# A fused block with 256 expert gathers: head 0's expert numbers written in two eights, two groups of queries moved between the sums, gather buffers in another order, tile 1's steps at other ticks, the last gather in half rows

## The chip, the cores and the metric

The kernel runs on one core of one Trainium2 chip. The metric is device time in microseconds (us) of one execution; lower is better. All arithmetic is float32.

## The reference

Two transformer blocks run one after the other on 256 tokens of width 1024. Only the end of the second block matters here, the feed-forward layer with product keys. Each token has 8 heads. For each head, the query is scored against two tables of 128 keys, the best 16 of each table are combined to 256 candidates, and the best 16 candidates name 16 of 16,384 experts. An expert is a row `u` and a row `v` of 1024 floats each.

```python
def peer_ffn(h, w_q, keys1, keys2, u, v):
    ...
        q = (hc @ w_q).reshape(-1, PEER_HEADS, PEER_KEY_DIM).astype(jnp.float32)
        s1 = jnp.einsum('chd,nd->chn', q[..., :half], k1)
        s2 = jnp.einsum('chd,nd->chn', q[..., half:], k2)
        v1, i1 = lax.top_k(s1, PEER_TOPK)
        v2, i2 = lax.top_k(s2, PEER_TOPK)
        cand_s = (v1[..., :, None] + v2[..., None, :]).reshape(*v1.shape[:-1], PEER_TOPK * PEER_TOPK)
        cand_i = (i1[..., :, None] * N_KEYS + i2[..., None, :]).reshape(*i1.shape[:-1], PEER_TOPK * PEER_TOPK)
        best_s, best_pos = lax.top_k(cand_s, PEER_TOPK)
        expert = jnp.take_along_axis(cand_i, best_pos, axis=-1)
        g = jax.nn.softmax(best_s, axis=-1)
        act = jax.nn.gelu(jnp.einsum('cd,chkd->chk', hc, u[expert],
                                     preferred_element_type=jnp.float32), approximate=False)
        wgt = (g * act).astype(hc.dtype)
        return jnp.einsum('chk,chkd->cd', wgt, v[expert])
```

## The kernel before

The 256 tokens are two tiles of 128 rows, tile 0 and tile 1. The first half of the program computes the first block and the attention of the second block for tile 0. Then the expert stage of tile 0 starts, and the rest of tile 1 (its projections, its attention, its output projection, its queries) is threaded between the expert steps.

**A set.** The unit of the expert stage is a set `n` (0 to 255): one expert for each of 128 tokens. Sets 0 to 127 are tile 0's (head 0's 16 experts are sets 0 to 15, head 1's are 16 to 31, and so on), sets 128 to 255 are tile 1's. A set passes four engines: GpSimd (POOL) issues a gather (L2431) that fetches 128 rows of 8 KB, `u` and `v` side by side, 1 MB in all; VectorE (DVE) takes the dot product of the `u` half with the token (L2244); ScalarE (ACT) takes its gelu (L1439); GpSimd writes a diagonal matrix with gelu times softmax weight (L2403); TensorE (PE) multiplies the `v` half by that diagonal and adds it to a bank of psum (L1036, the set's "sum", four matmul records of 512 columns).

**Buffers.** A gather needs a free buffer, a slot. `slot_table` hands out the slots in order: `SLOTS` is 7 at first, and `JOIN` says before which set more are added (one before set 7, three before 88, two before 118). A slot comes free when its sum is done (`pe_used`). The first slots are a buffer of their own (`first_slot`), then halves of weight buffers that are free once their last user on TensorE is done: two in `wr0` after the output projection (`wout_ready`), two in `wr1` after the queries of heads 2 and 3 (`pq01`), two in `wr2` after the queries of heads 6 and 7 (`pq03`), then `xc`, free after `h2_done`. `pq02` and `pq03` are the queries of heads 4, 5 and 6, 7 of tile 0; both read `wr2`.

**GpSimd's queue.** GpSimd issues in program order, and a wait of one gather holds all that follow. Before it issues a gather into a slot whose last set was `before`, it has written the diagonals up to `before + LEAD`, that is `before + 2`:

```python
                while before is not None and laid <= before + LEAD:
                    expert_diagonal(laid)
                    laid += 1
```

**Ticks.** The order on TensorE, ScalarE and VectorE is written by hand. `until(tick)` on VectorE does the dot products of all sets below `tick`; on ScalarE the gelus of sets below `tick - 1`; on TensorE the sums of sets below `tick - 2`. Between calls of `until` stand the steps of tile 1. `att_tick(step)` places the ten steps of its attention, `T_TURN` the two transposes `mb1` and `ma1` of its result, `T_WOUT` its output projection and `T_QUERY` its queries.

**Expert numbers.** `route(head, step)` on VectorE is the selection for one head in 17 steps. Steps 0 to 6 find the best 8 candidates, steps 7 to 9 (L2158 to L2165) the next 8, steps 10 to 16 (L2168 to L2192) turn the 16 positions into expert numbers; step 16 signals `eid_done`. Head 0 runs through all steps before the first gather; head 1's steps 0 to 8 stand before the dot product of set 0 and the rest between those of sets 0 to 4. The weights of head 0's softmax (`softmax_sum`, L2200 to L2206, signal `norm_done`) stand before the dot product of set 2, and the first diagonal waits for them.

## Time and profile before

| | |
|---|---|
| median of 3 runs | 1464.35 us (1464.03 to 1465.04) |
| the profiled execution, its own time | 1460.45 us |
| its span in the profile | 1458.4 us |
| mean granted TensorE clock | 0.985 of full speed |
| HBM read over the span | 424.05 MB |
| TensorE busy | 1330.5 us (91%) |
| VectorE busy | 860.1 us (59%) |
| GpSimd busy | 430.8 us (30%) |
| ScalarE busy | 284.8 us (20%) |

Busy time is that of the whole span. All times in the rows below count from the start of the span. "DMA share" is the mean busy share of the core's 16 DMA engines, and GB/s is what they moved; a stretch at a share of 1.00 or 1.01 and about 425 GB/s is one in which they never ran dry. One gather of 1,048,576 bytes at 425 GB/s is 2.47 us.

### The profile page before, as it was taken

The numbers are of one execution on the slowest core, as the hardware profiler recorded it, in microseconds if no ns is written. First come the engines' busy times: TensorE is split into PE (matmuls) and PEld (weight loads), VectorE is DVE, ScalarE is ACT, GpSimd is POOL, SyncE is SP. The second block draws the span as 40 slices with busy tenths as digits, with TensorE's granted clock in tenths as the row PEclk, the third lists the DMA queues.
The fourth block names the chain that finished last, engine by engine and source line by source line (L and its number), as shares of the span: only waits on it lengthen the run. The fifth ranks groups of instructions, "written<-read, shape, count | busy, mean of one in ns | idle before, by whom it ended". The sixth has DMA issues, their size and how long they took to land.

```text
span 1458.4 us, 14811 instructions
## 1 busy us (share of the span) xinstructions
PE 1330.5 (91%) x5269; PEld 863.7 (59%) x5269; DVE 860.1 (59%) x2028; ACT 284.8 (20%) x680; POOL 430.8 (30%) x547
## 2 busy tenths in 40 slices
PE   7999999999999999999998999988998777777786
PEld 6887888898868777767566644445552222222222
DVE  3558461236117888844357668775666677766654
ACT  2123101032010000013423124531221112111101
POOL 0002000120001000000005445664556555655551
PEclk9999999999999999999899999998999999999999
DMA  8343533311366888767339999998999999999995
GB/s 284 118 173 116 218 130 115 116 59 58 128 231 241 290 291 297 267 216 289 116 124 420 423 424 422 422 417 353 425 425 426 425 426 425 426 425 426 426 425 250
DMA packets 119369, 426.10 MB, mean 292 GB/s; under 512 B 10674, under 2 KB 34680, under 8 KB 84224
## 3 DMA queue, kind: packets, MB, share of 16 engines
q0 software_dynamic: 37072, 270.59, 44.4%
q1 hardware_dynamic: 82224, 154.57, 29.5%
q8 instruction: 42, 0.69, 0.2%
q14 instruction: 31, 0.25, 0.0%
HBM read 424.05 MB, written 1.08 MB: 292 GB/s over the span
## 4 chain that ended last, share of the span: by engine, by line
PE 61%; DMA 29%; ACT 3%; DVE 3%; issue 2%; POOL 2%; SPq 0%; POOLq 0%; DVEq 0%; ACTq 0%
PE psum L563 30%; DMA wr<-peer_uv,arena 13%; DMA arena<-peer_uv,arena 8%; PE psum L1036 7%; DMA xc<-peer_uv,arena 4%; PE psum L811 4%; DMA first_slot<-peer_uv,arena 3%; PE psum L888 2%; PE psum L787 2%; PE psum L861 1%; PE psum L608 1%; PE psum L1186 1%; POOL arena L2403 1%; PE psum L1054 1%; PE psum L1007 1%
## 5 line engine op out<-in xcount | busy, mean ns | idle before, releaser
L563 PE MATMUL psum<-hT,wr 128*128 128x256 f32 x1792 | 389.8, 379 | 1.6 <-DVE hT L1592 1.6
L563 PEld LDWEIGHTS psum<-hT,wr 128*128 128x128 f32 x1792 | 339.8, 190 | 50.8 <-issue 5.3
L1036 PE MATMUL psum<-wr,arena 128*128 128x512 f32 x576 | 279.3, 615 | 39.5 <-POOL arena L2403 39.3
L2244 DVE CUSTOM_DVE_ANT_0 wr<-psum,wr 128x1024 f32<-128x1024 f32 x144 | 176.1, 1223 | 118.2 <-DMA wr<-peer_uv,arena 117.6
L1036 PEld LDWEIGHTS psum<-wr,arena 128*128 128x128 f32 x576 | 102.9, 193 | 180.8 <-issue 179.9
L2403 POOL TENSOR_SCALAR arena<-cst,arena 128x128 f32<-128x128 f32 x256 | 121.9, 476 | 193.5 <-ACT arena L1439 187.7
L2431 POOL DMA_INDIRECT wr<-peer_uv,arena x144 | 143.9, 999 | 75.0 <-PE psum L1036 47.4
L1036 PE MATMUL psum<-arena 128*128 128x512 f32 x256 | 125.8, 616 | 33.6 <-POOL arena L2403 33.6
L1439 ACT ACTIVATE arena<-arena 128x1 f32<-128x1 f32 x256 | 50.9, 202 | 504.3 <-DVE arena L2244 503.9
L2244 DVE CUSTOM_DVE_ANT_0 arena<-psum,arena 128x1024 f32<-128x1024 f32 x64 | 78.4, 1224 | 55.1 <-DMA arena<-peer_uv,arena 55.1
L1036 PEld LDWEIGHTS psum<-arena 128*128 128x128 f32 x256 | 44.0, 190 | 111.4 <-issue 111.2
L2386 POOL TENSOR_TENSOR arena<-arena 128x512 f32<-128x512 f32 x11 | 16.9, 1536 | 217.4 <-DVE arena L1607 217.4
L1887 DVE SCALAR_TENSOR_TENSOR arena<-arena,csil 128x512 f32<-128x512 f32 x96 | 79.2, 825 | 3.0
L1605 DVE TENSOR_SCALAR arena<-psum,vec 128x256 f32<-128x256 f32 x68 | 29.7, 479 | 86.4 <-PE psum L563 78.5
L1607 DVE SCALAR_TENSOR_TENSOR arena<-psum,vec,arena 128x255 f32<-128x255 f32 (+1 forms) x160 | 69.8, 477 | 2.8
L2431 POOL DMA_INDIRECT arena<-peer_uv,arena x64 | 64.2, 1003 | 15.7 <-issue 12.4
L2374 POOL TENSOR_TENSOR arena<-arena,xc 128x512 f32<-128x512 f32 x12 | 17.0, 1445 | 167.6 <-PE psum L710 133.7
L2431 POOL DMA_INDIRECT first_slot<-peer_uv,arena x24 | 24.0, 1000 | 129.7 <-DVE arena L2192 116.5
L811 PE MATMUL psum<-wr,arena 128*128 128x512 f32 x128 | 55.6, 592 | 0.0
L563 PE MATMUL psum<-arena,wr 128*128 128x256 f32 x256 | 55.4, 379 | 0.0
L1036 PE MATMUL psum<-first_slot,arena 128*128 128x512 f32 x96 | 47.7, 621 | 7.1 <-POOL arena L2403 7.1
L563 PEld LDWEIGHTS psum<-arena,wr 128*128 128x128 f32 x256 | 48.6, 190 | 7.0 <-issue 0.5
(332 smaller groups left out, 1548.4 us busy)
## 6 DMA issues: line engine op xcount, KB each, us to landing
wr<-in_w_in SPq DMA_DIRECT2D x22, 2048.0 KB, 8.3
arena<-in_w_ada SPq DMA_DIRECT2D x12, 2048.0 KB, 9.7
wr<-in_w_up SPq DMA_DIRECT2D x22, 1024.0 KB, 7.8
arena<-piece SPq DMA_DIRECT2D x16, 1024.0 KB, 9.0
wr<-in_w_down SPq DMA_DIRECT2D x5, 2048.0 KB, 9.5
wr<-in_w_a_out SPq DMA_DIRECT2D x2, 2048.0 KB, 8.0
wr<-in_w_b_out SPq DMA_DIRECT2D x2, 2048.0 KB, 8.4
wr<-in_w_o SPq DMA_DIRECT2D x2, 2048.0 KB, 7.7
```

Source lines behind the costliest of these rows:

```text
L563: mm = nc.tensor.matmul(bank[p % 4][:, f * S:(f + 1) * S], slot(i)[:, k, c:c + P], act[:, k, :], start=k == 0, stop=k == KT - 1)
L787: mm = nc.tensor.matmul(bank[4 + 2 * n + t][:, :], sgb[:, k, t * P:(t + 1) * P], slot(23 + n)[:, k, :], start=k == 0, stop=k == KT - 1)
L811: mm = nc.tensor.matmul(bank[4 + 2 * n + t][:, :], act_ffn[:, f, t * P:(t + 1) * P], slot(i)[:, row, n * BANK:(n + 1) * BANK], start=f == ...
L888: mm = nc.tensor.matmul(o[:, f * P:(f + 1) * P], w[:, k, f * P:(f + 1) * P], hT[:, k, tiles_of[t]], start=k == 0, stop=k == KT - 1)
L1036: mm = nc.tensor.matmul(bank[(6, 0)[t] + half][:, :], diag[:, n % DIAGS, :], gring[slot_of][:, D + half * BANK:D + (half + 1) * BANK], sta ...
L1439: A_(col, dots[:, t, c:c + 1], ACT.Gelu).then_inc(s["gelu_done"], 1)
L1605: ins = V.tensor_scalar(dst[:, n, :], src[:, n, :], w, None, ALU.mult)
L1607: ins = V.scalar_tensor_tensor(out=dst[:, n, back:S], in0=src[:, n, 0:S - back], scalar=w, in1=dst[:, n, back:S], op0=ALU.mult, op1=ALU.add)
L1887: ins = V.scalar_tensor_tensor(out=part, in0=ada[j % 2][:, k, :], scalar=csil[:, k:k + 1], in1=part, op0=ALU.mult, op1=ALU.add)
L2244: V.tensor_tensor_reduce(gring[slot_of][:, 0:D], h2[t], gring[slot_of][:, 0:D], 1.0, 0.0, ALU.mult, ALU.add, dots[:, t, c:c + 1]).then_inc ...
L2403: G.tensor_scalar(diag[:, n % DIAGS, :], ident, wgt[:, t, c:c + 1], gsoft[:, t, c:c + 1], ALU.mult, ALU.mult).then_inc(s["diag_done"], 1)
L2431: G.indirect_dma_start(gring[slot_of], None, A["peer_uv"], bass.IndirectOffsetOnAxis(ap=eid[:, t, c:c + 1], axis=0)).then_inc(g_in[slot_of ...
```

## The change

1. Head 0's steps 10 to 16 run in two parts of 8 experts. The first part stands between steps 6 and 7, the second after step 9. `eid_done` counts one more from then on. Gather 0 waits for the first, gather 8 for the second.
2. On TensorE, `pq02` and `pq03` with their key scores stand between the sums of sets 0 to 5 and not ahead of them.
3. The slots come in another order: `first_slot`, two of `wr0`, `xc`, two of `wr1`; `SLOTS` is 6, and the two of `wr2` join before set 8.
4. Nearly all ticks of tile 1's steps are moved: the projections later (index rows behind `until(9)` and not `until(3)`), the attention at 32, 36, 41, 45, 50, 54, 59, 63, 68, 72 and not at 30, 35, ... 75, `T_TURN` 76 for 77, `T_WOUT` 80 for 78, `T_QUERY` 95 for 94. Three sums stand between the transposes `mb1` and `ma1`.
5. The last set, 255, is fetched by two gathers of 4 KB per row, first the `u` half, then the `v` half, each with a semaphore of its own.

The diff, cut to its core:

```diff
-SLOTS, DIAGS, LAG, LEAD = 7, 8, 2, 2
+SLOTS, DIAGS, LAG, LEAD = 6, 8, 2, 2
-T_TURN, T_WOUT, T_QUERY = 77, 78, 94
+T_TURN, T_WOUT, T_QUERY = 76, 80, 95
 def att_tick(step):
-    return 30 + 5 * step
+    return 32 + 9 * step // 2
-JOIN = {SLOTS: 1, 88: 3, 118: 2}
+JOIN = {8: 2, 88: 3, 118: 2}
...
-            for j in range(1, 4):
-                peer_queries(0, j)
-                key_scores(0, j)
-
+            peer_queries(0, 1)
+            key_scores(0, 1)
             until(3)
+            peer_queries(0, 2, 4)
+            until(5)
+            peer_queries(0, 3, 6)
+            key_scores(0, 2)
+            until(8)
+            key_scores(0, 3)
+            until(9)
             index_rows(1)
...
             until(T_TURN)
             turn("mb1", 1, 4, 11)
+            until(T_TURN + 3)
             turn("ma1", 1, 0, 12)
...
-            for step in range(STEPS):
+            for step in range(7):
                 route(0, step)
+            for step in range(10, STEPS):
+                route(0, step, slice(0, PK // 2))
+            for step in range(7, 10):
+                route(0, step)
+            for step in range(10, STEPS):
+                route(0, step, slice(PK // 2, PK))
             forget_logits(1)
...
-            until(att_tick(UNITS + 1) + 2)
+            until(att_tick(UNITS + 1) + 3)
             branch_rows(1, 0)
-            until(att_tick(UNITS + 1) + 5)
+            until(att_tick(UNITS + 1) + 6)
             branch_norm(1, 0)
-            until(T_TURN + 2)
+            until(T_TURN + 4)
             gain_evac(1)
...
                 elif n == 3:
+                    pool.wait_ge(s["h2_done"], 1)
+                elif n == 4:
                     pool.wait_ge(s["pair_ready"], filled("pq01"))
-                elif n == 5:
+                elif n == 8:
                     pool.wait_ge(s["pair_ready"], filled("pq03"))
-                elif n == SLOTS:
-                    pool.wait_ge(s["h2_done"], 1)
...
+                    for half in range(2):
+                        G.indirect_dma_start(gring[slot_of][:, half * D:(half + 1) * D], None, A["peer_uv"].rearrange("e (s n) -> (e s) n", s=2),
+                                             bass.IndirectOffsetOnAxis(ap=last_eid[:, half:half + 1], axis=0)).then_inc(last_in[half], 16)
```

What GpSimd has in its queue at the start of the expert stage, before (DMA rows are gathers, TENSOR_SCALAR rows are diagonals; the first row is gather 0):

```order
L2431 DMA first_slot<-peer_uv,arena 128x2048 [waits eid_done]
L2431 DMA wr0<-peer_uv,arena 128x2048 [waits wout_ready]
L2431 DMA wr0<-peer_uv,arena 128x2048
L2431 DMA wr1<-peer_uv,arena 128x2048 [waits pair_ready]
L2431 DMA wr1<-peer_uv,arena 128x2048
L2431 DMA wr2<-peer_uv,arena 128x2048 [waits pair_ready]
L2431 DMA wr2<-peer_uv,arena 128x2048
L2431 DMA xc<-peer_uv,arena 128x2048 [waits h2_done]
L2403 TENSOR_SCALAR arena<-cst,arena 128x128 [waits gelu_done,norm_done]
L2403 TENSOR_SCALAR arena<-cst,arena 128x128 [waits gelu_done] x2
L2431 DMA first_slot<-peer_uv,arena 128x2048 [waits pe_used]
```

and of the change:

```order
L2466 DMA first_slot<-peer_uv,arena 128x2048 [waits eid_done]
L2466 DMA wr0<-peer_uv,arena 128x2048 [waits wout_ready]
L2466 DMA wr0<-peer_uv,arena 128x2048
L2466 DMA xc<-peer_uv,arena 128x2048 [waits h2_done]
L2466 DMA wr1<-peer_uv,arena 128x2048 [waits pair_ready]
L2466 DMA wr1<-peer_uv,arena 128x2048
L2433 TENSOR_SCALAR arena<-cst,arena 128x128 [waits gelu_done,norm_done]
L2433 TENSOR_SCALAR arena<-cst,arena 128x128 [waits gelu_done] x2
L2466 DMA first_slot<-peer_uv,arena 128x2048 [waits pe_used]
L2433 TENSOR_SCALAR arena<-cst,arena 128x128 [waits gelu_done]
L2466 DMA wr0<-peer_uv,arena 128x2048 [waits pe_used]
L2466 DMA wr2<-peer_uv,arena 128x2048 [waits eid_done,pair_ready]
```

Before, eight gathers stand ahead of the first one that waits for a sum (`pe_used`), now six; gather 8 now waits for `pq03` (its `pair_ready`).

TensorE at the same place, of the change. L1009 are the matmuls of a pair of queries (`wr1`: `pq01`, `wr2`: `pq02` and `pq03`), L1020 the key scores, L1041 the sums:

```order
L1009 MATMUL psum<-hT,wr1 128x128 x15
L1020 MATMUL psum<-keysT,arena 128x128 [waits bank_free1,bank_free0]
L1020 MATMUL psum<-keysT,arena 128x128
L1020 MATMUL psum<-keysT,arena 128x128 [waits bank_free2]
L1020 MATMUL psum<-keysT,arena 128x128
L1041 MATMUL psum<-first_slot,arena 128x512 [waits diag_done,g_in0]
L1041 MATMUL psum<-first_slot,arena 128x512
L1009 MATMUL psum<-hT,wr2 128x128 [waits w_in2,bank_free3]
L1009 MATMUL psum<-hT,wr2 128x128 x7
L1041 MATMUL psum<-wr0,arena 128x512 [waits diag_done,g_in1]
L1041 MATMUL psum<-wr0,arena 128x512
L1009 MATMUL psum<-hT,wr2 128x128 x8
```

Before, both pairs of `wr2` with their key scores stood whole ahead of the first sum; now half of `pq02` stands behind sum 0 and half behind sum 1, and `pq03` in the same way around sum 3.

TensorE at `T_TURN` (tile 1's attention is done; L852 is a transpose, L991 the last attention product), before:

```order
L991 MATMUL psum<-arena 128x64 [waits bank_free1]
L991 MATMUL psum<-arena 128x64 x3
L852 MATMUL psum<-cst,xc 128x128 [waits bank_free0,xn_done]
L852 MATMUL psum<-cst,xc 128x128 x3
L852 MATMUL psum<-cst,xc 128x128 [waits bank_free1,xn_done]
L852 MATMUL psum<-cst,xc 128x128 x3
L1036 MATMUL psum<-wr1,arena 128x512 [waits diag_done,g_in3]
```

and of the change (L854 are the transposes, L1197 the output projection):

```order
L854 MATMUL psum<-cst,xc 128x128 [waits bank_free0,xn_done]
L854 MATMUL psum<-cst,xc 128x128 x3
L1041 MATMUL psum<-wr0,arena 128x512 [waits diag_done,g_in2]
L1041 MATMUL psum<-wr0,arena 128x512
L1041 MATMUL psum<-xc,arena 128x512 [waits diag_done,g_in3]
L1041 MATMUL psum<-xc,arena 128x512
L1041 MATMUL psum<-wr1,arena 128x512 [waits diag_done,g_in4]
L1041 MATMUL psum<-wr1,arena 128x512
L854 MATMUL psum<-cst,xc 128x128 [waits bank_free1,xn_done]
L854 MATMUL psum<-cst,xc 128x128 x3
L1041 MATMUL psum<-wr1,arena 128x512 [waits diag_done,g_in5]
L1197 MATMUL psum<-arena,hT 128x256 [waits p_in0,bank_free1,bank_free0]
```

The second transpose waits for `xn_done`, the normed rows from VectorE; three sums now stand ahead of it.

## Rows read from the trace of the kernel before

**Rows 1.** The page: DMA share in 40 slices, in tenths.
```profile
DMA  8343533311366888767339999998999999999995
```

**Rows 2.** Windows: busy of PE, PEld, DVE, ACT, POOL, then clock, DMA share, GB/s.
```profile
764.00:766.00 2.00, 2.00 (x21) 2.00 (x20) 1.90 (x12) 0.41 (x2) 1.70 (x2) 1.00 0.83 221
766.00:980.00 214.00, 203.21 (x734) 111.54 (x732) 155.98 (x448) 74.39 (x176) 114.91 (x156) 0.97 1.01 422
989.00:1003.00 14.00, 13.92 (x39) 8.39 (x40) 7.94 (x20) 0.81 (x4) 4.35 (x7) 0.80 0.65 235
1003.00:1440.00 437.00, 358.02 (x905) 145.75 (x904) 286.89 (x723) 74.72 (x222) 251.62 (x341) 1.00 1.01 425
```

**Rows 3.** Timeline of VectorE at the start: start, duration, instruction, idle before.
```profile
757.46 0.09 DVE L2158 MATCH_VALUE_LOAD arena<-arena 128x8 f32 x1
...
758.99 0.17 DVE L2168 TENSOR_SCALAR arena<-arena 128x16 uint32<-128x16 uint32 x1
...
759.48 0.76 DVE L2177 TENSOR_TENSOR arena<-arena,cst 128x256 f32<-128x256 f32 x2
...
763.01 0.47 DVE L2130 MAX8 arena<-arena 128x8 f32<-128x128 f32 x2
...
768.34 1.21 DVE L2244 CUSTOM_DVE_ANT_0 first_slot<-psum,first_slot 128x1024 f32<-128x1024 f32 x1
...
771.53 1.23 DVE L2244 CUSTOM_DVE_ANT_0 wr<-psum,wr 128x1024 f32<-128x1024 f32 x1 [1.28 <-DMA wr<-peer_uv,arena]
...
773.96 0.23 DVE L2206 TENSOR_SCALAR arena<-arena,stat 128x16 f32<-128x16 f32 x1
...
790.54 1.23 DVE L2244 CUSTOM_DVE_ANT_0 first_slot<-psum,first_slot 128x1024 f32<-128x1024 f32 x1 [0.28 <-DMA first_slot<-peer_uv,arena]
```

**Rows 4.** Timeline of GpSimd at the start.
```profile
762.51 1.03 POOL L2431 DMA_INDIRECT first_slot<-peer_uv,arena  x1 [116.46 <-DVE arena L2192]
...
771.61 0.94 POOL L2431 DMA_INDIRECT wr<-peer_uv,arena  x1 [3.06 <-PE psum L1007]
...
775.07 1.73 POOL L2403 TENSOR_SCALAR arena<-cst,arena 128x128 f32<-128x128 f32 x3
779.33 1.01 POOL L2431 DMA_INDIRECT first_slot<-peer_uv,arena  x1 [2.53 <-PE psum L1036]
```

**Rows 5.** Timeline of TensorE: queries and scores, the first sum, the second transpose.
```profile
767.49 3.84 PE L1007 MATMUL psum<-hT,wr 128*128 128x128 f32 x32
771.81 0.72 PE L1018 MATMUL psum<-keysT,arena 64*128 64x128 f32 x8 [0.47 <-ACT arena L1351]
775.67 3.38 PE L1036 MATMUL psum<-first_slot,arena 128*128 128x512 f32 x4 [3.14 <-POOL arena L2403]
...
989.08 1.12 PE L852 MATMUL psum<-cst,xc 128*128 128x128 f32 x4 [8.82 <-DVE xc L2077]
```

**Rows 6.** The chain that ended last, in order of time: start, us, what.
```profile
783.25 1.72 PE psum L1036 x4
784.97 1.78 PE psum L888 x16
```

**Rows 7.** DMA issues from 760 to 776 us: median us from issue to landing.
```profile
first_slot<-peer_uv,arena POOLq DMA_INDIRECT x1, 5.5
```

**Rows 8.** VectorE around the second transpose (the dot product of set 79, the norm).
```profile
987.20 1.23 DVE L2244 CUSTOM_DVE_ANT_0 xc<-psum,xc 128x1024 f32<-128x1024 f32 x1 [1.14 <-DMA xc<-peer_uv,arena]
...
988.54 0.49 DVE L2077 TENSOR_SCALAR xc<-xc,stat 128x512 f32<-128x512 f32 x1
```

**Rows 9.** Timeline of GpSimd: gather 83, which waits for sum 75.
```profile
993.89 1.00 POOL L2431 DMA_INDIRECT wr<-peer_uv,arena  x1 [7.51 <-PE psum L1036]
```

**Rows 10.** Timeline of all engines at the end: sets 254 and 255.
```profile
1446.72 1.96 PE L1036 MATMUL psum<-arena 128*128 128x512 f32 x4 [0.47 <-POOL arena L2403]
1446.92 1.23 DVE L2244 CUSTOM_DVE_ANT_0 arena<-psum,arena 128x1024 f32<-128x1024 f32 x1 [1.19 <-DMA arena<-peer_uv,arena]
...
1449.15 1.96 PE L1036 MATMUL psum<-arena 128*128 128x512 f32 x4 [0.47 <-POOL arena L2403]
```

## Prediction before the run

> **What bounds the kernel now.** I read the page first: from slice 22 on the DMA engines are busy in nearly every slice [rows 1]. The windows say it sharper. From 766 to 980 us and from 1003 to 1440 us the DMA share is 1.01, at 422 and 425 GB/s [rows 2]. TensorE is busy in those stretches too, but it is DMA that never has a pause, so the expert stage is a queue of transfers: its end is the start of the first gather, plus the bytes, plus every pause of the DMA engines, plus the tail behind the last landing. One gather takes 1,048,576 bytes / 425 GB/s = 2.47 us. The change moves no byte into or out of the stage, so only start, pauses and tail can change. There is one pause in the kernel before: from 989 to 1003 us the share is 0.65, which is 4.9 us of standstill, and 235 GB/s, which by bytes is 14 x (1 - 235/425) = 6.3 us lost [rows 2]. Waits of the other engines matter only where they hold a gather back so long that the queue runs dry.
>
> **Start: gather 0 is earlier.** Steps 10 to 16 of head 0 start at 758.99 and the gather that waits for them at 762.51, 3.52 us later [rows 3, 4]. Between a signal and GpSimd's next instruction I take 0.28 us: the last queries end at 767.49 + 3.84 = 771.33 and gather 5, which waits for them, starts at 771.61 [rows 4, 5]. So the seven steps take 3.24 us. In halves, the three pairs of 256 elements (0.76 us a pair, L2177 and two like it) become pairs of 128, for which the pair of 0.47 us stands [rows 3]: 3 x 0.29 = 0.87 us less, 2.37 us for a part. The first part now starts where steps 7 to 9 started, at 757.46. Gather 0 goes out at 757.46 + 2.37 + 0.28 = 760.1 us, **2.4 us earlier**. VectorE pays for it: two parts are 4.74 us where 3.24 us stood, so all behind them is 1.5 us later.
>
> **Start: only six gathers are covered.** Before, eight gathers stood ahead of the first that needs a sum; gather 8 waited for sum 0 and started at 779.33, that is 775.67 + 3.38 + 0.28 [rows 4, 5]. Now it is gather 6 that waits for sum 0. When does sum 0 come? Not earlier because the queries of heads 4 to 7 are out of its way: the first diagonal also waits for head 0's softmax weights on VectorE, done at 773.96 + 0.23 = 774.19 [rows 3]. In the change, the dot product of set 0 starts at 768.34 + 1.5 = 769.84; the next, without the wait of 1.28 us (its gather lands 2.4 us earlier), at 769.84 + (771.53 - 1.28 - 768.34) = 771.75; the weights are ready 774.19 - 771.53 = 2.66 us later, at 774.4. From the first diagonal to sum 0 it was 775.67 - 775.07 = 0.6 us [rows 4, 5]: sum 0 starts at about 775.1. TensorE has stood idle since about 762, so the sum runs at 1.2 GHz. It did so before as well, after only 3.14 us of idle time: 3.38 us, where a sum at 2.4 GHz takes 1.72 [rows 5, 6]. Sum 0 ends at 778.5, gather 6 goes out at 778.8.
>
> From issue to landing a gather into an empty queue takes 5.5 us [rows 7]. The six gathers land until 760.1 + 5.5 + 5 x 2.47 = 778.0; gather 6 lands at 778.8 + 5.5 = 784.3 where 780.4 was possible: **a pause of 3.9 us**.
>
> **Start: gathers 7 and 8.** Gather 7 waits for sum 1, gather 8 for `pq03`. Between them TensorE now has to do, in this order, half of `pq02`, sum 1, the other half, sum 2, half of `pq03`, sum 3, the other half. A half is a sixteenfold row, 1.78 us, as the projection halves are; a sum is 1.72 us [rows 6]. I add 0.4 us for the rest of the time at 1.2 GHz. Sum 1 ends at 778.5 + 2.2 + 1.7 = 782.4, gather 7 goes out at 782.7 and lands at 788.2 where 786.8 was possible: 1.4 us. `pq03` ends at 782.4 + 3 x 1.78 + 2 x 1.72 = 791.2; sums 2 and 3 are free long before, but gather 8 stands in front of gathers 9 to 11 in GpSimd's queue and holds them all. It goes out at 791.5 and lands at 797.0 where 790.7 was possible: **6.3 us**. In sum 3.9 + 1.4 + 6.3 = 11.6 us of pauses, less the 2.4 us gained: the start is **9.2 us later**. Before, an unbroken row of landings would have brought gather 8 at 762.51 + 5.5 + 8 x 2.47 = 787.8; its dot product really started at 790.54, when the slowest of the DMA engines had landed it [rows 3]. A pause lets the slow engine catch up, so by last landings the loss may be only 797.0 - 790.5 = 6.5 us. That is the lower bound; at full clock all along it is 2.1 us less (sum 0 1.66 us shorter, the 0.4 us gone).
>
> **The pause at 989 us.** Its cause is in the trace: TensorE waits 8.82 us for the normed rows before the second transpose [rows 5]; the norm (988.54) stands on VectorE behind the dot product of set 79 (987.20) [rows 8], and sum 75 stands behind the transpose, so gather 83 leaves only at 993.89, after 7.51 us of waiting [rows 9]. In the change the norm stands behind set 77 and the transpose behind sum 76. A sum starts 1449.15 - 1446.92 = 2.23 us after the dot product of its set [rows 10] and takes 1.72, so sum 76 ends 3.95 us after dot 76, that is 1.5 us after dot 77 starts; the norm ends 1.34 + 0.49 = 1.8 us after dot 77 starts [rows 8]. The wait shrinks from 8.82 us to well under 1. What is late next is the output projection: it waits for the evacuation behind dot 79, at 4.9 + 1.2 + 0.7 = 6.9 us after dot 77; half a quarter (1.7) and sum 78 (1.7) follow, which ends at 10.3 where 6.4 is natural, 3.9 us late. With eight slots a gather may go out up to 8 x 2.47 - 5.5 = 14.3 us after the landing of the set whose slot it takes, and goes out after 3.95 + 0.28 = 4.2 us: 10 us are spare. Sum 75 was beyond that before: it ended at 993.6, where dot 75, four sets ahead of 987.2, gives 977.3 + 3.95 = 981.3, so 12.3 us late. Now 3.9 us fit. **The pause goes: -6.3 us** by bytes, at least -4.9 by the share.
>
> **The tail.** Set 255 in half rows lets its dot product start half a gather earlier, 1445.7. Its sum could then start 2.23 us later, at 1447.9, but sum 254 holds TensorE until 1446.72 + 1.72 = 1448.44 [rows 6, 10]. It started at 1449.15: **-0.7 us**. The extra gather, 1 us of GpSimd, goes out with ten others queued ahead and costs nothing there. No gather of half rows is in the trace.
>
> Here the Trainium skill speaks against the change ("DMA: Bandwidth & Descriptors", sections "Bandwidth" and "Anatomy of one DMA"): transfers are to be batched to 1 MiB or more, and its fit gives each GpSimd-issued DMA a fixed 2.0 us. If the second half paid that in full behind the first, the last `v` rows would land at 1448.9 and the tail would gain 0.2 us and not 0.7, for a sum 0.5 us higher. In the queue of this kernel 1 MB transfers land 2.47 us apart at 425 GB/s, with no fixed part to be seen, so I don't expect it.
>
> **What else is moved, at nothing.** Queries and scores of heads 4 to 7, 2 x (3.84 + 0.72) in the old place [rows 5], now lie behind sum 0, and TensorE has 9 us more to do there; but the gathers come 9 us later too. The tightest place I find is gather 18, behind sum 10: sum 4 starts at about 794.3 (its diagonal stands behind gathers 8 and 9), and until sum 10 ends there are seven sums, two short steps of about 0.7 and three projection halves, 12.0 + 1.4 + 5.3 us: 813.0. The gather lands at 818.8, due at 797.0 + 10 x 2.47 = 821.7: 2.9 us are spare. If that cover goes, each microsecond of delay is a microsecond of the end. Attention steps stand 4.5 sets apart and not 5; in that stretch the DMA share was 1.01 throughout [rows 2], and from the rows I can't exclude a late gather there, up to some 3 us. SyncE's weight pieces follow the queries and projections that free them and stay ahead of use by the same counts of sets.
>
> **Sum.** +9.2 - 6.3 - 0.7 = **+2.2 us** on the profiled execution's own 1460.45 us: 1462.65. That execution was 3.9 us under the median of 1464.35, and I put the difference on the median: 1466.5. Bounds of the same mechanism: 6.5 - 2.1 - 6.3 - 0.7 = -2.6 us and 9.2 - 4.9 - 0.7 = +3.6 us, with 1 us more if the clock stays low longer: 1461.8 to 1469. A measurement of this kernel tells about 0.2% from no change, 2.9 us.
>
> **Rivals.**
> *Faster: gather 8 is not late.* If TensorE had `pq03` done before gathers 0 to 7 have drained, only the pause at gather 6 is left: -2.4 + 3.9 - 6.3 - 0.7 = -5.5 us, 1458.9. It decides at the issue of gather 8: before 786.4 us the change is faster by over 0.2%. For it: VectorE's chain to sum 0 is my reconstruction. Against: three sums stand in between, and even at 2.4 GHz throughout gather 8 goes out at 789.4. 15%. With no pause at all, -9.4 us, 1455.0: 5%.
> *Slower: the pause at 989 stays.* If another wait in that place (the statistics on ScalarE, the evacuation behind set 79) holds the sums more than 10 us, it is 9.2 - 0.7 = +8.5 us, 1472.9. Against: the count above leaves 6 us. 10%.
> *Slower: a new pause behind gather 14 or in the closer attention*, worth about 3 us: 1469.6. The spare 2.9 us at gather 18 speak for it, the 1.01 of before against. 15%.
> *My forecast*, 55%: two thirds of its own range lie within 0.2%, one third above.
>
> **Numbers.** Faster: 15 + 5 = 20%. Within 0.2%: 38 of the 55, and 2 of the new pause, 40%. Slower: 17 + 10 + 13 = 40%. The range takes in the faster rival and the new pause, and leaves out "no pause at all" and most of "the pause stays": 1458.5 to 1471.5.
>
> **What would show it.** Gather 0 at about 760.1; gather 6 at about 778.8, gather 8 at about 791.5, with its wait on TensorE's L1009; DMA share well under 1 around 779 to 783 and 788 to 794; sum 0 of 3.4 us at half the clock. Around set 77 the second transpose waits under 1 us, and the share stays at 1 until the end. The last sum starts right behind the one before. I am wrong if gather 8 leaves before 787, if the share dips after 797, or if the weights of head 0 are ready much before 774.4.

## Result and the profile after

The changed kernel takes 1468.01 us (median of 20 runs, 1464.25 to 1471.53), the kernel before on the same chips 1464.13 us (20 runs). The ratio is 1.0024, interval 1.0016 to 1.0033: 3.9 us slower, where +2.2 us was forecast. The profiled execution took 1470.77 us, its span is 1468.8 us at a mean clock of 0.982.

The two profiles can't be set beside each other as they are. Up to head 0's route both programs are the same, but the first step of that route starts at different times in the two executions (VectorE's timeline, before and after):

```profile
753.06 0.49 DVE L2130 MAX8 arena<-arena 128x8 f32<-128x128 f32 x2 [1.27 <-ACT arena L1351]
```
```profile
757.14 0.49 DVE L2147 MAX8 arena<-arena 128x8 f32<-128x128 f32 x2 [1.29 <-ACT arena L1362]
```

The 4.08 us between them are not the change. In the twelve profiles of the experiments below, which share the program up to that point, this step starts between 752.3 and 757.0 us. Every time of after is therefore compared less 4.08 us. Compared so, after's span ends 6.3 us behind that of before (1468.8 - 4.08 - 1458.4), and not 3.9: the profile of before was a fast one behind this step too (experiment 1), so the size of the change is taken from the medians.

**The start.** GpSimd's timeline of after (start, duration, instruction, idle before it and what ended it) answers to [rows 4]:

```profile
764.26 1.03 POOL L2466 DMA_INDIRECT first_slot<-peer_uv,arena  x1 [116.66 <-DVE arena L2213]
...
770.60 0.94 POOL L2466 DMA_INDIRECT wr<-peer_uv,arena  x1 [0.30 <-issue]
778.46 0.89 POOL L2433 TENSOR_SCALAR arena<-cst,arena 128x128 f32<-128x128 f32 x2 [6.92 <-DVE arena L2227]
...
783.08 1.00 POOL L2466 DMA_INDIRECT first_slot<-peer_uv,arena  x1 [2.61 <-PE psum L1041]
...
787.32 1.00 POOL L2466 DMA_INDIRECT wr<-peer_uv,arena  x1 [2.75 <-PE psum L1041]
796.11 0.94 POOL L2466 DMA_INDIRECT wr<-peer_uv,arena  x1 [7.79 <-PE psum L1009]
```

Gather 0 leaves at 764.26, less 4.08 is 760.2 (forecast 760.1). Gather 6 leaves at 779.0 (778.8), gather 7 at 783.2 (782.7), gather 8 at 792.0 (791.5), and its wait of 7.79 us ends on the query line L1009, that is on `pq03`. TensorE in the same stretch, which answers to [rows 5]:

```profile
779.05 3.75 PE L1041 MATMUL psum<-first_slot,arena 128*128 128x512 f32 x4 [12.76 <-POOL arena L2433]
782.60 2.73 PE L1009 MATMUL psum<-hT,wr 128*128 128x128 f32 x16
785.16 1.88 PE L1041 MATMUL psum<-wr,arena 128*128 128x512 f32 x4
...
793.88 1.95 PE L1009 MATMUL psum<-hT,wr 128*128 128x128 f32 x16
```

Sum 0 runs 3.75 us after 12.76 us of idle time, between two halves of queries come sums, and the last half ends at 795.8. The windows show what the DMA engines made of it, and what became of the pause at 989 us (they answer to [rows 2]; columns as there):

```profile
770.00:785.00 15.00, 5.95 (x19) 3.91 (x20) 14.62 (x51) 0.81 (x4) 4.22 (x7) 0.54 0.83 334
785.00:802.00 17.00, 14.56 (x78) 9.72 (x78) 5.06 (x19) 4.68 (x11) 6.14 (x8) 1.00 0.58 207
800.00:1440.00 640.00, 550.73 (x1597) 254.02 (x1595) 435.56 (x1141) 152.00 (x398) 361.33 (x488) 0.98 1.01 423
989.00:1003.00 14.00, 11.26 (x29) 4.66 (x27) 10.62 (x27) 5.83 (x15) 7.94 (x12) 0.88 1.01 421
```

By bytes at 425 GB/s the start lost 15 x (1 - 334/425) + 17 x (1 - 207/425) = 3.2 + 8.7 = 11.9 us (forecast 11.6). The clock of 0.54 in the first window is TensorE's lower level, 1.2 GHz: the granted clock was 0.50 from 771 to 783 us. It fell while TensorE stood idle (from 766.3 us on), and sum 0 still ran at it. Behind 800 us there is no pause any more: 1.01 for 640 us, and 1.01 where before had 0.65.

**The tail.** VectorE and TensorE at the end, as in [rows 10]:

```profile
1455.62 1.22 DVE L2268 CUSTOM_DVE_ANT_0 arena<-psum,arena 128x1024 f32<-128x1024 f32 x1 [1.20 <-DMA arena<-peer_uv,arena]
...
1456.84 1.22 DVE L2268 CUSTOM_DVE_ANT_0 arena<-psum,arena 128x1024 f32<-128x1024 f32 x1
```
```profile
1457.85 3.67 PE L1041 MATMUL psum<-arena 128*128 128x512 f32 x8 [0.47 <-POOL arena L2433]
```

The dot product of set 255 stands directly behind that of set 254, and sums 254 and 255 are one unbroken row of eight matmuls, where before had two rows 2.43 us apart. So each mechanism came as forecast, and the times of the start to half a microsecond. The open question is the arithmetic: 9.2 less 6.3 less 0.7 gives 2.2 us and not 3.9. What is a pause of the DMA engines worth?

### The profile page after: what moved, and what is told of

It reads as the page before. It is cut to its first block, busy times and chain, and to the rows that moved or that the text cites. A ratio compares the mean times of both kernels' runs of the same rounds, so it can differ in the third digit from the quotient of the medians.

```text
span 1468.8 us, 14829 instructions
## 1 busy us (share of the span) xinstructions
PE 1333.3 (91%) x5269; PEld 866.5 (59%) x5269; DVE 862.8 (59%) x2041; ACT 289.1 (20%) x683; POOL 431.2 (29%) x548
## 3 DMA queue, kind: packets, MB, share of 16 engines
q1 hardware_dynamic: 82224, 154.57, 29.2%
## 4 chain that ended last, share of the span: by engine, by line
PE 61%; DMA 28%; DVE 4%; ACT 3%; issue 2%; POOL 2%; SPq 0%; DVEq 0%; POOLq 0%; ACTq 0%
PE psum L565 30%; DMA wr<-peer_uv,arena 16%; DMA arena<-peer_uv,arena 10%; PE psum L1041 8%; PE psum L813 4%; PE psum L890 2%; PE psum L789 2%; DMA first_slot<-peer_uv,arena 2%; PE psum L863 2%; PE psum L1009 2%; PE psum L610 1%; PE psum L1059 1%; PE psum L872 1%; POOL arena L2433 1%; DVE wr L2268 1%
## 5 line engine op out<-in xcount | busy, mean ns | idle before, releaser
L1041 PE MATMUL psum<-wr,arena 128*128 128x512 f32 x572 | 275.5, 609 | 41.8 <-POOL arena L2433 41.6
L1041 PEld LDWEIGHTS psum<-wr,arena 128*128 128x128 f32 x572 | 101.6, 192 | 181.4 <-issue 180.5
L1041 PE MATMUL psum<-arena 128*128 128x512 f32 x256 | 124.2, 611 | 30.4 <-POOL arena L2433 30.4
L1041 PEld LDWEIGHTS psum<-arena 128*128 128x128 f32 x256 | 44.0, 189 | 107.5 <-issue 107.1
L1041 PE MATMUL psum<-first_slot,arena 128*128 128x512 f32 x100 | 50.1, 625 | 18.1 <-POOL arena L2433 18.1
L1041 PE MATMUL psum<-xc,arena 128*128 128x512 f32 x96 | 48.8, 632 | 8.4 <-POOL arena L2433 8.3
L813 PE MATMUL psum<-wr,arena 128*128 128x512 f32 x128 | 55.6, 592 | 0.0
```

The costliest lines, as they stand in the source:

```text
L813: mm = nc.tensor.matmul(bank[4 + 2 * n + t][:, :], act_ffn[:, f, t * P:(t + 1) * P], slot(i)[:, row, n * BANK:(n + 1) * BANK], start=f == ...
L1041: mm = nc.tensor.matmul(bank[(6, 0)[t] + half][:, :], diag[:, n % DIAGS, :], gring[slot_of][:, D + half * BANK:D + (half + 1) * BANK], sta ...
```

## Experiments

All were timed beside the kernel before on the same chips, 12 runs each (the last 9). Medians of before were 1463.81, 1463.92, 1463.66 and 1463.34 us in the four groups. "Theory A" is the prediction's: every microsecond of idle DMA share is a microsecond of the end. "Theory B": the end is set by the slowest of the 16 engines, which lags behind the others, and a pause that only the engines ahead of it notice costs nothing. "Lag" is how far the last engine is behind the mean of the 16.

**1. The two eights alone**, on the kernel before.

```diff
-            for step in range(STEPS):
+            for step in range(7):
                 route(0, step)
+            for step in range(10, STEPS):
+                route(0, step, slice(0, PK // 2))
+            for step in range(7, 10):
+                route(0, step)
+            for step in range(10, STEPS):
+                route(0, step, slice(PK // 2, PK))
             forget_logits(1)
```

> The kernel before with part 1 of the change alone: head 0's expert numbers in two eights; queries, slots, ticks and last set as before. If the start of the queue is all that counts: gather 0 goes out 2.4 us earlier (2.37 + 0.28 us behind step 6), gather 5 still waits for the queries of heads 6 and 7 and goes out at about 771.6 (due at 772.5, so no pause), gather 8 at about 779.3 (due at 779.9), so no pause of the DMA engines opens and the end is 2.4 us earlier: ratio 0.9984. Rival: VectorE's extra 1.5 us delays the first sum and gather 8 opens a pause of about 1 to 2 us: ratio 0.9990 to 1.000.

Measured: 1462.87 us, ratio 0.9997 (0.9986 to 1.0007). The gain of 2.4 us isn't there; at most 2.0 us lie in the interval. Its route starts at 755.22 us, 2.16 later than that of before. TensorE and GpSimd in its timeline:

```profile
766.20 3.84 PE L1007 MATMUL psum<-hT,wr 128*128 128x128 f32 x32 [1.83 <-DVE small L1983]
```
```profile
775.28 1.07 POOL L2442 DMA_INDIRECT wr<-peer_uv,arena  x1 [6.90 <-PE psum L1007]
...
784.22 1.01 POOL L2442 DMA_INDIRECT first_slot<-peer_uv,arena  x1 [3.81 <-PE psum L1036]
```

VectorE's extra 1.5 us delay the forget logits (L1983), which free the psum bank that `pq02` needs. Gather 5, which waits for `pq03`, leaves 20.1 us behind the route's start, and gather 8 29.0 us. In the profile of before it was 18.6 (771.61 - 753.06, [rows 4]) and 26.3. But that profile stands alone. In the five of experiments 2, 5, 6, 9 and 10, whose program is that of before up to there, gather 5 leaves 21.8 to 22.1 us behind the route's start and gather 8 29.2 to 29.9. TensorE and GpSimd in that of experiment 6, whose route starts at 752.74:

```profile
768.27 0.89 PE L1018 MATMUL psum<-keysT,arena 64*128 64x128 f32 x8 [2.21 <-ACT arena L1351]
769.09 5.26 PE L1007 MATMUL psum<-hT,wr 128*128 128x128 f32 x32
```
```profile
774.62 0.93 POOL L2431 DMA_INDIRECT wr<-peer_uv,arena  x1 [6.40 <-PE psum L1007]
...
782.68 1.00 POOL L2431 DMA_INDIRECT first_slot<-peer_uv,arena  x1 [3.17 <-PE psum L1036]
```

The key scores behind `pq02` wait 2.21 us for ScalarE's copy, 0.47 in the profile of before, and `pq03` takes 5.26 us and not 3.84: behind that wait the granted clock was 0.50 (770 to 772 us), in before 1.00. What holds the copy the profile doesn't tell. Beside these five, the two eights send gather 8 only 0.2 to 0.9 us earlier, because it still waits for what stands behind `pq03`; that is about the gain that the times show.

**2. The turn's ticks alone**, on the kernel before.

```diff
-T_TURN, T_WOUT, T_QUERY = 77, 78, 94
+T_TURN, T_WOUT, T_QUERY = 76, 80, 95
...
+            until(T_TURN + 3)
             turn("ma1", 1, 0, 12)
...
-            until(att_tick(UNITS + 1) + 5)
+            until(att_tick(UNITS + 1) + 3)
             branch_norm(1, 0)
-            until(T_TURN + 2)
+            until(T_TURN + 4)
```

> The kernel before with only the place around the second transpose changed: three sums between the two transposes, the norm two sets earlier, T_TURN 76, T_WOUT 80, T_QUERY 95; start, attention ticks and last set as before. The pause of the DMA engines at 989 to 1003 us should go. Theory of the mean (the end moves by what the DMA share lost): -4.9 us, ratio 0.9967. Theory of the slowest engine (the pause had let the slowest of the 16 DMA engines catch up with the others, and the last landing is its landing): the lag stays and the end moves by only -2 to -3 us, ratio 0.9980 to 0.9986, with a longer drain at the end. If the pause had cost nothing: 1.000.

Measured: 1461.74 us, 0.9989 (0.9980 to 0.9998). The pause is gone (the windows show 423 GB/s from 980 to 1020 us), and TensorE waits only 1.02 us for the normed rows:

```profile
992.68 0.66 PE L852 MATMUL psum<-cst,xc 128*128 128x128 f32 x4 [1.02 <-DVE xc L2078]
```

But taking 6.3 us of lost bytes away gave 2.1 us (0.3 to 2.9). Theory A, which wanted 4.9, is out; theory B wanted 2.0 to 3.0.

**3. The queries of heads 4 to 7 ahead of sum 0 again**, in the changed kernel, with ScalarE's copies that belong to them; all else as changed.

```diff
-            until(3)
-            peer_queries(0, 2, 4)
-            ...
+            for j in range(1, 4):
+                peer_queries(0, j)
+                key_scores(0, j)
             until(9)
```

> The changed kernel with the queries and key scores of heads 4 to 7 ahead of the first sum again (on TensorE and ScalarE), all else as changed. If gather 8 is late because its slot waits for those queries behind three sums: gather 8 goes out right behind gather 7 (about 782 in the time of before), only the pause of 3.9 us at gather 6 is left, DMA share back at 1 from 785 on, and the kernel is 6 to 8 us faster than the changed one: ratio to before 0.9972 by the mean, 0.9988 if the slowest engine keeps its lag. Rival (the slots' order itself, six slots, makes the loss): gather 6 to 8 late as in the changed kernel, ratio 1.001 to 1.003.

Measured: 1462.96 us, 0.9999 (0.9988 to 1.0009). By the ratios to before that is 3.7 us under the changed kernel (4.7 us by its second timing, experiment 8), less than the 6 to 8 us expected. GpSimd's timeline (the route starts at 753.00 there):

```profile
780.73 1.00 POOL L2455 DMA_INDIRECT first_slot<-peer_uv,arena  x1 [1.95 <-PE psum L1041]
783.69 1.00 POOL L2455 DMA_INDIRECT wr<-peer_uv,arena  x1 [1.47 <-PE psum L1041]
785.00 0.95 POOL L2455 DMA_INDIRECT wr<-peer_uv,arena  x1 [0.30 <-issue]
```

Gather 8 leaves 32.0 us behind the route's start; in the changed kernel it is 39.0. Placing the queries between the sums is what makes the changed kernel slower.

**4. The parts that should help, together**: two eights, the turn's ticks and the half rows on the kernel before, with its seven slots and its order of queries. The diffs are those of 1, 2 and 10.

> The kernel before with the parts that should gain and none that should lose: two eights, the three sums between the transposes, the last set in half rows; slots, queries and attention ticks as before. Sum of the terms: -2.4 - 4.9 - 0.7 = -8.0 us by the mean, ratio 0.9945; with the lag of the slowest engine kept -5.5 us, ratio 0.9962. If the start gain is an illusion: -2.5 to -5.5 us.

Measured: 1460.21 us, 0.9976 (0.9964 to 0.9988): 3.6 us faster than before. The sums of 8.0 and 5.5 us are both missed; it is the third case of the expectation, in which the start gains next to nothing.

**5 and 6. A squeeze of the queue, narrow and wide.** Both are the kernel before with one wait of GpSimd made longer, so that one gather leaves late and the DMA engines run short of work for a moment, in the steady part of the stage, far from any other step.

```diff
-                while before is not None and laid <= before + LEAD:
+                while before is not None and laid <= ((197 - 1) if n == 200 else before + LEAD):
...
-                    pool.wait_ge(s["pe_used"], before + 1)
+                    pool.wait_ge(s["pe_used"], 197 if n == 200 else before + 1)
```

The first pair of lines writes the diagonals that the longer wait needs ahead of it. The wide one has 199 for 197 in both.

> The kernel before with one squeeze added: gather 200 waits for sum 196 instead of sum 193, and nothing else is changed. When sum 196 ends, about 4 us after the last engine has landed set 196, the slowest of the 16 DMA engines still has sets 197 to 199 to bring, 7.4 us, and the new gather needs about as long to reach it. The faster engines are some 4 us ahead and run dry. Theory A (the stage's end is set by the mean of the engines, so that every idle share of the 16 counts): the DMA share dips by 2 to 3 us around 1300 us and the time is 2 to 3 us longer than before, ratio 1.0014 to 1.0020. Theory B (the end is set by the slowest engine, and what the others lose while it works on is free): the share dips alike, the drain at the end is steeper (the engines finish closer together), and the time is that of before, 0.9995 to 1.0005.

> The kernel before with the squeeze of the earlier run made wider by two sets: gather 200 waits for sum 198 instead of sum 196. It then leaves 2 x 2.47 = 4.9 us later, and by then even the slowest engine has brought all that was queued. Theory A (mean of the engines): the first squeeze should have cost about 3 us, this one 8 us, ratio 1.0055. Theory B (the end is set by the slowest engine, which a squeeze costs nothing until it outlasts that engine's lag): the first squeeze cost nothing and stopped just short of the point, this one is beyond it by 3 to 5 us: 1466.5 to 1469, ratio 1.0018 to 1.0035, although the idle share is 8 us. Ratio 1.000 would mean that neither is right and pauses here cost nothing at all.

Measured: narrow 1464.07 us, 1.0003 (0.9989 to 1.0016); wide 1469.16 us, 1.0036 (1.0022 to 1.0050). The windows of before, of the narrow and of the wide squeeze, in this order (1450 us on: the drain of the last sets; before had drained by 1447):

```profile
1300.00:1320.00 20.00, 15.22 (x32) 5.12 (x30) 14.11 (x41) 4.41 (x11) 11.38 (x16) 1.00 1.01 426
1440.00:1442.00 2.00, 1.47 (x5) 0.43 (x4) 0.86 (x2) 0.20 (x1) 0.45 (x1) 1.00 0.74 311
1442.00:1447.00 5.00, 4.05 (x9) 1.49 (x10) 2.55 (x5) 0.41 (x2) 0.90 (x2) 1.00 0.12 49
```
```profile
1300.00:1320.00 20.00, 7.87 (x17) 2.77 (x17) 13.38 (x40) 4.20 (x10) 9.36 (x13) 0.82 0.90 354
...
1450.00:1451.00 1.00, 0.87 (x2) 0.49 (x3) 0.67 (x1) 0.00 (x0) 0.00 (x0) 1.00 0.62 262
1451.00:1453.00 2.00, 1.53 (x4) 0.49 (x3) 0.82 (x3) 0.20 (x1) 0.45 (x1) 1.00 0.08 33
```
```profile
1300.00:1320.00 20.00, 7.68 (x16) 2.63 (x16) 10.48 (x33) 3.86 (x9) 9.38 (x12) 0.79 0.63 248
...
1450.00:1451.00 1.00, 1.00 (x4) 0.38 (x2) 0.92 (x2) 0.05 (x1) 0.00 (x0) 1.00 0.35 147
1451.00:1453.00 2.00, 1.53 (x5) 0.63 (x4) 0.89 (x1) 0.16 (x1) 0.45 (x1) 1.00 0.04 16
```

The narrow squeeze lost 20 x (1 - 354/426) = 3.4 us of bytes and costs 0.15 us (-1.6 to +2.3), which is nothing that can be measured. The wide one lost 20 x (1 - 248/426) = 8.4 us and costs 5.5 (3.2 to 7.3). Theory A, by which all 3.4 and 8.4 us count, is out. The times alone don't show the threshold of theory B: if three fifths of every pause counted, 2.0 and 5.0 us, both would lie in the intervals.

The traces decide it. They hold the time of each of the 16 counts by which the 16 engines signal that a gather has landed. From gather 199, the last ahead of the squeeze, to gather 203 an unbroken row takes 4 x 2.47 = 9.9 us. In the narrow run the mean landing took 13.1 us (1309.9 to 1323.0) and the last one 10.3 (1313.5 to 1323.8); in the wide run 18.1 (1304.5 to 1322.6) and 15.1 (1308.5 to 1323.6). So the mean of the engines lost 3.2 and 8.2 us and the last engine 0.4 and 5.2, which is what the kernel paid. About 3 us were free in either; the lag fell from 3.6 to 0.8 us and from 4.0 to 1.0.

The drain shows the lag itself. In before, the engines finish on average at 1440 + 2 x 0.74 + 5 x 0.12 = 1442.1 us, and the last set lands at 1446.9 [rows 10]: the last engine is 4.8 us behind the mean. The counts of the last gather say 4.3 us. With the narrow squeeze the mean is 1450 + 0.62 + 0.16 = 1450.8 and the last dot product starts at 1452.75 (2.0 us behind); with the wide one 1450.4 and 1452.11 (1.7 us); by the counts 1.4 and 1.2 us. At the end of the changed kernel, after a long undisturbed stretch, the share is

```profile
1448.00:1450.00 2.00, 1.96 (x4) 0.67 (x4) 1.23 (x2) 0.20 (x1) 0.10 (x1) 1.00 0.75 311
1450.00:1458.00 8.00, 6.01 (x13) 2.21 (x14) 4.85 (x8) 0.61 (x3) 1.69 (x4) 1.00 0.14 58
```

so the mean is 1448 + 1.5 + 1.1 = 1450.6, and bytes still arrive about 7 us later (7.0 by the counts). But the length of the stretch doesn't set this number. The second profile of the same kernel (experiment 8) has

```profile
1448.00:1450.00 2.00, 1.64 (x4) 0.38 (x2) 1.15 (x2) 0.20 (x1) 0.45 (x1) 1.00 1.00 418
1450.00:1458.00 8.00, 6.37 (x14) 2.33 (x14) 4.92 (x8) 0.84 (x5) 1.34 (x4) 1.00 0.31 127
```

and a lag of 4.8 us by the counts; experiment 2, without the pause at 989 us, ends with 5.1. A pause lets the lag shrink: over before's pause at 989 us it fell from 2.4 to 0.5 us. Behind it the lag grows back, to 4.3 us at the end, and the last set pays it. The Trainium skill ("DMA: Bandwidth & Descriptors", section "Two DMAs through the same engine are not ordered") says that nothing orders transfers across the 16 engines. The drains agree: with the queue never empty, the engines drift several microseconds apart.

A single profile can't price such small pauses. Between 50 and 225 us behind the route's start, before and the kernels of experiments 5, 6, 9 and 10 run the same program and moved 422, 417, 423, 421 and 411 GB/s. At 425 GB/s that is 0.8 to 5.8 us lost of 175, as much as most of the effects here, so the prices come from the times and the profiles only show the mechanism.

**7. The pause put back into the changed kernel.**

```diff
-            until(T_TURN + 3)
             turn("ma1", 1, 0, 12)
```

> The changed kernel with the second transpose of the turn straight behind the first again (the wait for the sum of its set between them taken out); all else as in the changed kernel. The transpose then stands and waits for the normed rows, sums are held back, and the DMA engines pause around 990 us. Theory A (bytes or share lost count): +4.9 to +6.3 us on the changed kernel, ratio to it 1.0033 to 1.0043. Theory B (the slowest engine): the slowest engine was about 3.4 us behind the first at that place and catches up in the pause, so that 2 to 3.5 us come back, 1.0014 to 1.0024. If the wait between the transposes is not what removed the pause (the other moved steps did it), no dip at 990 us and a ratio of 1.000.

**8. The changed kernel once more**, beside it.

> The changed kernel once more, unchanged. If the 4 us by which its first profile was already late at the start of head 0's route is noise of single executions (the program up to there is the same in both kernels), this profile starts its route anywhere between 753 and 757 us, and from there to the end it takes 711 to 712 us as the first one did, where the kernel before took 705.5. If it belongs to the kernel, the route starts at 757 again. Ratio to before 1.0020 to 1.0030.

Measured: 1468.43 us with the pause, 1468.04 us without (to before 1.0031, 1.0017 to 1.0044, and 1.0031, 1.0019 to 1.0044). The route of the second starts at 756.64 and its span is 1468.5 us: 711.9 us from there to the end, as in the first profile (711.7). TensorE and the windows of the kernel with the pause:

```profile
998.00 1.12 PE L854 MATMUL psum<-cst,xc 128*128 128x128 f32 x4 [7.20 <-DVE xc L2092]
```
```profile
1000.00:1020.00 20.00, 20.00 (x57) 11.11 (x57) 12.09 (x28) 3.96 (x10) 11.63 (x15) 0.94 0.91 355
```

The transpose waits 7.20 us again and the queue loses 20 x (1 - 355/425) = 3.3 us of bytes, as much as in the narrow squeeze, and it costs 0.4 us by the medians, within the noise (the means of the 12 runs of each are equal to 0.1 us, with 1.5 us either way). So the wait between the transposes is what removes the pause, and in the changed kernel that is worth 1.5 us at most; even theory B, with 2 to 3.5 us, had it too large.

**9. Eight sets in half rows**, on the kernel before: sets 248 to 255, 16 gathers for 8.

```diff
+                    for half in range(2):
+                        G.indirect_dma_start(gring[slot_of][:, half * D:(half + 1) * D], None,
+                                             A["peer_uv"].rearrange("e (s n) -> (e s) n", s=2), ...)
```

> The kernel before with the last eight sets (248 to 255) each fetched by two gathers of half rows instead of one of whole rows, both waited for together: 8 gathers more, the same bytes. Theory: in a queue that is never empty a gather has no fixed part that counts, so the time is that of before, 0.9995 to 1.0010; GpSimd needs about 3 us a set there where 2.5 stand between landings, which its 10 us of lead cover. Rival, by the page's fixed part of 2.0 us for each gather: up to 16 us more, ratio 1.011, or 1.003 if a quarter of it is seen.

Measured: 1464.00 us, 1.0004 (0.9991 to 1.0017). The last dot products, each waiting for both halves:

```profile
1443.68 1.23 DVE L2254 CUSTOM_DVE_ANT_0 arena<-psum,arena 128x1024 f32<-128x1024 f32 x1 [1.23 <-DMA arena<-peer_uv,last_ids]
1446.13 1.23 DVE L2254 CUSTOM_DVE_ANT_0 arena<-psum,arena 128x1024 f32<-128x1024 f32 x1 [1.22 <-DMA arena<-peer_uv,last_ids]
1448.58 1.23 DVE L2254 CUSTOM_DVE_ANT_0 arena<-psum,arena 128x1024 f32<-128x1024 f32 x1 [1.21 <-DMA arena<-peer_uv,last_ids]
```

They stand 2.45 us apart, as with whole rows (2.43 us between the last such sets of experiment 10). The fixed 2.0 us for each DMA of the Trainium skill's fit ("DMA: Bandwidth & Descriptors", section "Anatomy of one DMA") doesn't show in this full queue.

**10. Set 255 alone in half rows**, on the kernel before.

> The kernel before with set 255 alone in half rows. Its dot product starts when the first half has landed, and sum 255 directly behind sum 254: 0.7 us earlier in the profile, ratio 0.9995. Rival: the second half arrives a fixed part later, sum 255 waits for it, and nothing is gained, 1.0000. The interval of the times can't tell these apart; the profile's last two sums can.

Measured: 1464.68 us, 1.0007 (0.9993 to 1.0021). The profile decides, as expected: sums 254 and 255 are one row, `1450.32 3.67 ... x8`. The 0.7 us are too small for the times, which neither show nor exclude them.

**11. The best parts, with the forget logits earlier**: `forget_logits(1)` stands between the first eight and steps 7 to 9.

> The version of the best parts (before, with head 0's experts in two eights, the turn's steps moved, the last set in half rows), and in it the three small VectorE steps of the forget logits moved from behind the second eight to behind the first, so that TensorE no longer waits 1.8 us for the bank that they free. Theory: the queries of the last heads end 1.8 us earlier, gather 5 leaves 1.8 us earlier and its 0.6 us of pause goes; gather 8 stays where VectorE's chain to sum 0 puts it. 0 to 0.6 us better than without the move: ratio to before 0.9970 to 0.9976. Rival: gather 8 is what counts, and the whole is unchanged, 0.9976.

Measured: 1459.06 us, 0.9976 (0.9964 to 0.9988). By the ratio it is the version of experiment 4: the rival's number. Gather 5 leaves 19.6 us behind the route's start and not 20.1: 0.5 us earlier, not 1.8. The wait for the bank is gone, and the key scores behind `pq02` wait for ScalarE's copy instead, 1.92 us where it was 0.47:

```profile
769.60 0.72 PE L1021 MATMUL psum<-keysT,arena 64*128 64x128 f32 x8 [1.92 <-ACT arena L1358]
```

So the bank was not all that held the queries in experiment 1.

**12. The first sum early**, on top of 11.

```diff
-                        for step in (range(9), (9, 10), (11, 12), (13, 14), (15, 16))[n]:
+                        for step in ((), (), range(7), range(7, 12), range(12, STEPS))[n]:
                             route(1, step)
-                    if n == LAG:
+                    if n == 1:
```

> The version of the best parts with the logits moved, and in it the routing of head 1 taken out of the way of the first dot products: its steps stand behind sets 2 to 4 instead of 0 to 4, and head 0's softmax weights are scaled ahead of dot product 1 instead of 2. In the version without this, dot product 0 started at 771.66 us, some 2 us after its rows had landed, TensorE idled 3.16 us for the first diagonal at half the clock, and gather 8 left at 782.77, at a rate that leaves 1 to 2 us of pause. Theory: sum 0 starts 3 us earlier, gather 8 leaves in time and the start has no pause behind gather 5: 1 to 2.5 us better than without, ratio to before 0.9958 to 0.9972. Rival: sum 0 is held by the queries of the last heads on TensorE, or head 1's routing is now late for gather 16, and nothing is gained or something lost, 0.9976 to 1.000.

Measured: 1459.18 us, 0.9968 (0.9956 to 0.9980), which can't be told from experiment 11. The theory fell in the profile. Sum 0 starts 23.6 us behind the route's start, with VectorE's change and without it. GpSimd shows why:

```profile
777.16 0.94 POOL L2457 DMA_INDIRECT xc<-peer_uv,arena  x1 [0.30 <-issue]
778.14 1.32 POOL L2424 TENSOR_SCALAR arena<-cst,arena 128x128 f32<-128x128 f32 x3
783.18 1.00 POOL L2457 DMA_INDIRECT first_slot<-peer_uv,arena  x1 [3.73 <-PE psum L1042]
```

With seven slots the first diagonal stands in GpSimd's queue directly behind gather 7, which stands behind gather 5 and its wait for `pq03`. VectorE's weights have been ready for 7.8 us. Only with six slots, as in the changed kernel, is GpSimd free, and there the first diagonal does wait for VectorE (6.92 us, L2227, above).

## Why the prediction was right or wrong

- *Start, by issue times*: right to 0.5 us at every gather; lost bytes 11.9 us where 11.6 were forecast. Experiment 3 shows that the queries between the sums are the cause.
- *Start, as a price*: +9.2 us was too much. After's dot product of set 8 starts at 801.85 us, less 4.08 is 797.8, 7.2 us behind 790.54 [rows 3]. The prediction named this bound ("by last landings", +6.5) and did not take it. Its rows also came from an execution with a faster start than usual. From 7 to 50 us behind the route's start before's profile moved 373 GB/s (5.3 us lost), the five profiles with the same start 352 to 362 (6.4 to 7.4 us) and the three of kernels with the changed start 279 to 281 (14.6 to 14.8 us). Against its own profile the start costs 9.3 us or more, as forecast; against the usual execution 7.2 to 8.4.
- *The gain of the two eights*: 2.4 us in gather 0, as forecast. Alone, with seven slots, most or all of it is lost (experiment 1), since gather 8 leaves hardly earlier than in the five profiles with the old start. VectorE's extra 1.5 us were booked only against the first sum, and the bank of `pq02` behind the forget logits was not seen; moving the logits gave gather 5 only 0.5 us back (experiment 11).
- *The pause at 989 us*: it goes, for the reason given (experiments 2 and 7). **The step that failed is its price, "-6.3 us by bytes, at least -4.9 by the share"**: it measured -2.1 us alone, and -0.4 us, which is not different from nothing, in the changed kernel, whose pause would have lost 3.3 us of bytes. The bound from below was wrong in kind: both of its ends price the mean of the engines, and the catching up of the slowest, which the prediction used for the start, holds at every pause. It doesn't explain the whole: before's pause took the lag from 2.4 to 0.5 us, so of its 6.3 us some 4.5 should have been paid, and the times gave back 0.3 to 2.9.
- *Tail*: -0.7 us by the sums; seen in the profile, not in the times.
- *Sum*: 7.2 - 2.1 - 0.7 = +4.4 us with the sizes measured, against +3.9 measured. The two oversized terms had opposite signs, which is why +2.2 was not far off. The 1466.5 of the forecast was 1.5 us low, and the outcome fell just on the slower side of the line of 0.2%, whose interval (1.0016 to 1.0033) includes it.
- *Rivals*: gather 8 was late, the pause did not stay, no new pause came behind gather 14 (1.01 from 800 us on).
- *Putting the difference between the profile and the median on the median*: right. The profile of before was an early one; starts of the route scatter over 4 us. It was fast behind it too: 705.3 us from there to the end, where experiments 9 and 10, whose program differs only for the last sets, took 707.2 and 709.0.

Open: why the pause at 989 us was worth less than the last engine's loss in it (in experiment 2), and what in the changed kernel makes its pause of 3.3 us cheaper than theory B's estimate; both differences, about 2 us, are near what 12 runs can tell. Nor is it shown what holds ScalarE's copy behind `pq02` in the five profiles with the old start, when in that of before nothing did. Which transfers make one engine lag was not tried. Nor was the changed kernel's six slots with VectorE's weights early, the one place where experiment 12's idea could bear.

## What to carry to other kernels

A queue that never runs dry has no single end: price a pause by what its slowest engine loses, and read the lag from the drain (last landing minus mean finish). Here a lag of about 4 us made some 3 us of a squeeze free, and what came beyond was paid, so removing small pauses one by one gains little, while a large one must be kept from growing. Look at more than one profile before pricing a few microseconds: the rows of the start that the prediction used were those of one execution, 3 us ahead of the usual at gather 8. And when work is moved ahead of a long-known wait, look for what else stands behind the same engine: a psum bank, ScalarE's copy and GpSimd's queue order took back what the earlier gather had won.

## What was not expected of the hardware

With the queue full for 430 us the 16 DMA engines drift apart: in the last gather of before the last one was 4.3 us behind the mean, from 0.5 us after the pause at 989 us. In two executions of the changed kernel, whose queue had no pause for 640 us, it was 7.0 and 4.8 us. A squeeze 130 us before the end brought it to 1.4 and 1.2 us. Twice the number of gathers for the same bytes cost nothing measurable (1464.00 against 1463.66 us).
